# A decoder layer on one core: branch, output and query projections in three fp32r terms, norms between column groups

## What is computed

```python
def hybrid_mixer(h, ...):
    z = h @ p['w_in']                                   # q, k, v, gates, cq, ckv, kr, ga, gb
    ...                                                 # mLSTM branch gives hm
    y_a = hm @ p['w_branch_a']                          # 512 -> 1024
    ...                                                 # q_nope, k_nope, v from the latents
    o_lat = mla_attention(q_lat, q_rope, ckv, kr, ...)  # 8 heads; samples read 8192 cached tokens
    y_b = o_b @ p['w_branch_b']                         # 512 -> 1024
    y = (sigmoid(ga) * y_a + sigmoid(gb) * y_b) @ p['w_out']

def memory_attention(h, mem_k, mem_v, p):
    q = (h @ p['w_mq']).reshape(B, T, 4, 128)           # 1024 -> 512
    ...                                                 # softmax over 256 memory tokens
    return o @ p['w_mo']

def decoder_layer(x, ...):
    mem_k, mem_v = memory_kv(mem_prompt)                # norm of 256 memory rows, two 1024 -> 512
    x = x + rms_norm(hybrid_mixer(rms_norm(x, g_pre_mix)), g_post_mix)
    x = x + rms_norm(memory_attention(rms_norm(x, g_pre_mem)), g_post_mem)
    x = x + rms_norm(swiglu_ffn(rms_norm(x, g_pre_ffn)), g_post_ffn)
```

## Time and profile before

| | us |
|---|---|
| median of 3 runs (lowest, highest) | 2562.77 (2562.18, 2566.25) |
| the profiled execution | 2563.37 |
| its span, first to last instruction | 2561.5 |
| TensorE busy | 2334.8 (91%) |
| VectorE, ScalarE, GpSimd busy | 950.8, 735.4, 320.1 |
| mean granted TensorE clock | 0.961 of full |

### The profile page before, as it was taken

One profiled execution on the slowest core, in us unless ns is written; L12 is line 12 of the kernel. 1 busy time (PEld: TensorE's weight loads), 2 busy tenths in 40 slices (PEclk: granted clock), 3 DMA queues, 4 the chain that ended last, 5 costly groups with the idle time before them and its releaser, 6 DMA issues.

```text
span 2561.5 us, 36996 instructions
## 1 busy us (share of the span) xinstructions
PE 2334.8 (91%) x15757; PEld 1978.0 (77%) x15757; DVE 950.8 (37%) x1582; ACT 735.4 (29%) x1144; POOL 320.1 (12%) x384
## 2 busy tenths in 40 slices
PE   4999999999888899987999789958999999989994
PEld 4999899996444676665666456848999999989993
DVE  3352233334375554443110442464111111155556
ACT  5222222222343444434002112432111111144442
POOL 0000001102100477770020000000000000000000
PEclk9999999999899999998999899989999999999997
DMA  4123323332100577773141032021111111111121
GB/s 127 42 84 99 103 87 108 108 86 100 55 1 1 208 235 234 235 234 123 37 165 35 23 119 78 18 99 34 44 47 49 41 49 49 50 35 45 45 89 66
DMA packets 186468, 223.25 MB, mean 87 GB/s; under 512 B 18089, under 2 KB 148598, under 8 KB 185734
## 3 DMA queue, kind: packets, MB, share of 16 engines
q1 hardware_dynamic: 155238, 114.33, 14.5%
q0 software_dynamic: 31136, 107.56, 13.1%
HBM read 191.88 MB, written 29.98 MB: 87 GB/s over the span
## 4 chain that ended last, share of the span: by engine, by line
PE 77%; DVE 8%; POOL 5%; ACT 5%; issue 3%; DMA 2%; SPq 0%; POOLq 0%; ACTq 0%; DVEq 0%
PE ps L1410 21%; PE ps L937 17%; PE ps L1221 11%; PE ps L1610 10%; POOL mem L867 3%; POOL mem L868 2%; PE ps L1235 2%; PE ps L1240 2%; PE ps L1303 1%; DVE mem L2371 1%; PE ps L1107 1%; ACT mem L1831 1%; PE ps L1333 1%; DVE mem L2134 1%; DVE mem L2131 1%
## 5 line engine op out<-in xcount | busy, mean ns | idle before, releaser
L937 PE MATMUL ps<-stream_first,early_first 128*128 128x344 f32 x912 | 299.3, 328 | 4.3 <-DVE H_short L2087 3.0
L937 PE MATMUL ps<-H_short,early_first 128*128 128x344 f32 x912 | 294.7, 323 | 0.0
L937 PE MATMUL ps<-stream_first,ring_short 128*128 128x344 f32 x912 | 294.3, 323 | 0.0
L1221 PE MATMUL ps<-mem 128*128 128x344 f32 x960 | 282.5, 458 | 4.9 <-DMA mem<-w_out 4.3
L1221 PEld LDWEIGHTS ps<-mem 128*128 128x128 f32 x960 | 184.6, 193 | 102.5 <-issue 9.3
L1410 PE MATMUL ps<-stream_first,sel_short 128*128 128x344 f32 x1056 | 225.6, 322 | 16.0 <-DVE H_short L2664 16.0
L1410 PE MATMUL ps<-H_short,sel_short 128*128 128x344 f32 x1056 | 224.8, 321 | 0.0
L1410 PE MATMUL ps<-stream_first,ring_short 128*128 128x344 f32 x1056 | 223.4, 320 | 0.0
L1410 PEld LDWEIGHTS ps<-stream_first,sel_short 128*128 128x128 f32 x1056 | 178.2, 189 | 17.8 <-issue 13.4
L937 PEld LDWEIGHTS ps<-stream_first,early_first 128*128 128x128 f32 x912 | 174.9, 192 | 13.1 <-ACT mem L1740 6.1
L1410 PEld LDWEIGHTS ps<-H_short,sel_short 128*128 128x128 f32 x1056 | 179.5, 190 | 0.0
(11 more groups left out here) (422 smaller groups left out, 3389.8 us busy)
## 6 DMA issues: line engine op xcount, KB each, us to landing
ring_raw<-w_ffn_in SPq DMA_DIRECT2D x44, 512.0 KB, 3.6
ring_raw<-w_in SPq DMA_DIRECT2D x37, 512.0 KB, 3.8
ring_raw<-w_ffn_out SPq DMA_DIRECT2D x16, 704.0 KB, 4.5
branch_gates<-mem POOLq DMA_DIRECT2D x16, 516.0 KB, 4.6
mem<-branch_gates SPq DMA_DIRECT2D x2, 4128.0 KB, 14.5
chunks_apart<-mem POOLq DMA_DIRECT2D x12, 516.0 KB, 2.9
mem<-chunks_apart POOLq DMA_DIRECT2D x8, 768.0 KB, 5.7
residual_stream<-mem SPq DMA_DIRECT2D x8, 516.0 KB, 2.6
```

What stands on the lines that cost most here:

```text
L937: mm = pe.matmul(ps[:, bank, 0:TN], w[:, k], x[:, k, j * TN:(j + 1) * TN], start=(k == 0 and q == 0), stop=(k == KT - 1 and q == 2))
L1221: mm = pe.matmul(ps[0:m, s + j, 0:TN], w[:, k], x[:, j * TN:(j + 1) * TN], start=(k == 0), stop=(k == kts - 1))
```

## The change

- **a, b, out and mq become three-term fp32r products.** a, b and the first four out tiles use `product3` in thirds of 344 columns. Their inputs are split: Oo (for a) in the last decode unit, obT (for b) beside tiles 4 to 7 of a, the gated sum (for out) tile by tile behind the gates. The first two tiles of a stand ahead of the samples' product with w_uv, and their weights are loaded once the decode's values are done. The weights are split by ScalarE (`w_first`) and VectorE (`w_rest`).
- **The last four out tiles and mq run in column groups** of 384, 384 and 264: 24 products s = 0 to 23 (`group_product`), each one weight tile over one group with 24 matmuls; 0 to 11 are out, 12 to 23 mq. Their weights are split by ScalarE (`group_first`) and GpSimd (`group_rest`).
- **The norms run per group between these products.** ScalarE squares, GpSimd adds the squares (`add_square`), a matmul with ones sums them (`group_sum`), VectorE makes variance and reciprocal (`group_variance`), scales and adds the input (`add_input`), and later scales and splits the result (`stream_rest`).
- **Memory K and V stand behind mq**; kc, w_mv and vc are loaded later than before.
- **Three projection steps move into attention**: kn2 behind the first scores, kn3 and v2 behind the turns of units 0 and 1. Units 0 to 3 use one pair of banks.
- The one large SBUF tensor is allocated as two, and semaphores are renumbered.

```diff
-        N_A, N_B, N_OUT, N_MQ, N_MO, N_UP, N_DOWN = 0, 8, 16, 24, 28, 36, 80
+        N_A, N_B, N_OUT, N_MO, N_UP, N_DOWN = 0, 8, 16, 20, 28, 72
...
+        GROUP = [(0, 384), (384, 768), (768, T)]
+        SUMS = [("out", 0), ("in", 0), ("out", 1), ("out", 2), ("in", 1), ("in", 2)]
+        SUM_OUT = {4: 0, 8: 1, 12: 2}
+        SUM_IN = {7: 0, 13: 1, 17: 2}
+        QUADS = {5: (0, 0), 6: (0, 1), 9: (1, 0), 12: (1, 1), 14: (2, 0), 16: (2, 1)}
...
-        ATT = ["qr0", "qr1", "qn0", "rot0", "qn1", "rot1", "qn2", "qn3", "kn0", "kn1", "kn2", "kn3", "v0", "v1", "v2", "v3"]
+        ATT = ["qr0", "qr1", "qn0", "rot0", "qn1", "rot1", "qn2", "qn3", "kn0", "v0", "v1", "v3", "kn1", "kn2", "kn3", "v2"]
+        BESIDE = {0: "kn3", 1: "v2"}
...
+        def att_half(u):
+            return 1 if u < 4 else u % 2
...
@@ SyncE @@
+            sp.wait_ge(dec_values_done, NU)
+            for n in range(2):
+                load_w(N_A + n, w_a[:, :, n * P:(n + 1) * P])
             sp.wait_ge(pe_event, EV["o_T"])
...
+            for j in range(4):
+                load_group(j, w_o[:, :, (4 + j) * P:(5 + j) * P])
+            for j in range(4):
+                load_group(4 + j, w_q[:, :, j * P:(j + 1) * P])
...
+            sp.wait_ge(group_done, 24)
+            sp.dma_start(wmv, d["w_mv"][0].rearrange("(k p) m -> p k m", p=P)).then_inc(wmv_in, 16)
             for b in range(NB):
                 sp.dma_start(kc[:, b], kc_d[:, b]).then_inc(cache_keys_in, 16)
...
@@ GpSimd @@
+                pool.wait_ge(nrm_sq, SQ0 + n + 1)
+                if m:
+                    pool.tensor_tensor(acc, acc, gsq[n % 2][:, 0:w], ALU.add).then_inc(squares_added, 1)
...
+            for n in range(len(SQUARES)):
+                if n and SQUARES[n][2]:
+                    pool.wait_ge(squares_added, n)
+                add_square(n)
+                if n in (5, 8, 11, 12):
+                    group_rest((5, 8, 11, 12).index(n))
+                if SQUARES[n] in (("out", 2, 6), ("out", 2, 7), ("in", 1, 3), ("in", 1, 7)):
+                    group_rest(4 + (("out", 2, 6), ("out", 2, 7), ("in", 1, 3), ("in", 1, 7)).index(SQUARES[n]))
...
@@ TensorE @@
+            product3(N_A, H_rest[0:4], X_rest, ready=parts0, by=split_rest_ok)
+            product3(N_A + 1, H_rest[0:4], X_rest)
             pe.wait_ge(dve_event, EV["olat_ok"])
...
+            def group_product(s):
+                g, j = s // 12 * 4 + s % 4, s % 12 // 4
+                ...
+                if s >= 3:
+                    pe.wait_ge(group_evac, s - 2)
+                pe.wait_ge(group_rest_ok, g + 1)
+                for k in range(KT):
+                    if s >= 12 and s % 4 == 0:
+                        pe.wait_ge(split_rest_ok, parts0 + 16 + j * KT + k + 1)
+                    for q, (w, x) in enumerate(((ghi[g], first), (ghi[g], rest), (wlo[g % WSLOT], first))):
+                        mm = pe.matmul(ps[:, s % 3, 0:cols.stop - cols.start], w[:, k], x[k][:, cols],
+                                       start=(k == 0 and q == 0), stop=(k == KT - 1 and q == 2))
+                mm.then_inc(group_done, 1)
...
+            for s in range(24):
+                group_product(s)
+                if s in SUM_OUT:
+                    group_sum("out", SUM_OUT[s])
+                if s in QUADS:
+                    input_turn(*QUADS[s])
+                if s in SUM_IN:
+                    group_sum("in", SUM_IN[s])
...
@@ ScalarE, last decode unit @@
             for s in range(UPS):
                 dec_act(NB - 1, s, s == UPS - 1)
+                split_first(s, Alo[:, s], Oo[:, s])
+            act.wait_ge(pe_event, EV["o_T"])
+            w_first(0)
             act.wait_ge(dve_event, EV["wgt_arg"])
             act.activation(Wt, Wt, ACT.Exp, scale=SCALE)
             act.activation(Wself, Wself, ACT.Exp, scale=SCALE).then_inc(act_event, 1)
+            w_first(1)
...
@@ VectorE @@
             for s in range(UPS):
                 dec_dve(NB - 1, s, s == UPS - 1)
+                split_rest(s, Xlo[:, s], Oo[:, s], Alo[:, s])
...
+            group_variance("out", 0)
+            add_input(0, 0)
+            add_input(0, 1)
+            group_variance("in", 0)
+            group_variance("out", 1)
+            stream_rest(0)
+            add_input(1, 0)
+            add_input(1, 1)
+            group_variance("out", 2)
+            group_variance("in", 1)
+            add_input(2, 0)
+            stream_rest(1)
+            add_input(2, 1)
+            group_variance("in", 2)
+            stream_rest(2)
```

More of the change, by code:

```diff
@@ new lines, in group_sum @@
+            def group_sum(kind, j):
+                n = SUMS.index((kind, j))
+                c0, c1 = GROUP[j]
+                pe.wait_ge(squares_added, SQUARES.index((kind, j, KT - 1)) + 1)
+                if n:
+                    pe.wait_ge(nrm_var, NS0 + n)
+                else:
+                    pe.wait_ge(evac_act, 4)
+                acc = gacc_out[:, c0:c1] if kind == "out" else gacc_in[:, 0:c1 - c0]
+                pe.matmul(ps[:, 4, 0:c1 - c0], ones, acc, start=True, stop=True).then_inc(nrm_sum, 1)
@@ new lines, in _, with group_variance @@
+            for n in range(1, 2 * KT):
+                w_rest(n + 2)
+                gated(n)
+                if 4 <= n < 8:
+                    split_rest(n, ob_rest[:, n - 4], obT[:, n - 4], ob_first[(n - 4) // 2][:, n % 2])
+                if n >= KT + 2:
+                    sum_rest(n - KT - 2)
+            sum_rest(KT - 2)
+            sum_rest(KT - 1)
+            w_rest(N_OUT + 2)
+            w_rest(N_OUT + 3)
+            def group_variance(kind, j):
+                n = SUMS.index((kind, j))
+                r = grs_out if kind == "out" else grs_in
+                w = GROUP[j][1] - GROUP[j][0]
+                dve.wait_ge(nrm_sum, NS0 + n + 1)
+                step.step(dve.tensor_scalar(r[:, 0:w], ps[:, 4, 0:w], 1.0 / D, EPS, ALU.mult, ALU.add))
+                dve.reciprocal(r[:, 0:w], r[:, 0:w]).then_inc(nrm_var, 1)
@@ new lines, in add_input @@
+            def add_input(j, q):
+                cols = slice(*GROUP[j])
+                w = cols.stop - cols.start
+                dve.wait_ge(nrm_rstd, NS0 + SUMS.index(("out", j)) + 1)
+                for k in range(4 * q, 4 * q + 4):
+                    step.mark(dve.scalar_tensor_tensor(out=H[:, k, cols], in0=H[:, k, cols], scalar=gains[:, G_POSTMIX + k:G_POSTMIX + k + 1],
+                                                       in1=grs_out[:, 0:w], op0=ALU.mult, op1=ALU.mult))
+                step.join()
+                for k in range(4 * q, 4 * q + 4):
+                    dve.wait_ge(input_turned_again, j * KT + k + 1)
+                    dve.tensor_tensor(H[:, k, cols], H[:, k, cols], ps[:, X_BANK[k % 4], 0:w], ALU.add).then_inc(residual1_ok, 1)
@@ new lines, in stream_rest @@
+            def stream_rest(j):
+                cols = slice(*GROUP[j])
+                w = cols.stop - cols.start
+                r = grs_in[:, 0:w]
+                dve.wait_ge(nrm_rstd, NS0 + SUMS.index(("in", j)) + 1)
+                dve.wait_ge(residual1_ok, (j + 1) * KT)
+                for k in range(KT + 1):
+                    if k < KT:
+                        dve.scalar_tensor_tensor(out=A2[:, k, cols], in0=H[:, k, cols], scalar=gains[:, G_PREMEM + k:G_PREMEM + k + 1],
+                                                 in1=r, op0=ALU.mult, op1=ALU.mult).then_inc(group_raw_ok, 1)
+                    if k:
+                        split_rest(16 + j * KT + k - 1, sum_first[:, k - 1, cols], A2[:, k - 1, cols], Ahi[:, k - 1, cols])
```

667 lines of the change are left out of this document (411 added, 256 removed).

## The result

The changed kernel takes 2477.12 us (median of 4 runs, 2474.2 to 2478.61) beside 2564.51 us of the kernel before: ratio 0.9655, 95% interval 0.9637 to 0.9674. Forecast were 2468, between 2450 and 2500. The profiled execution took 2477.7 (span 2475.9), 85.7 less than that of before; the sum of the prediction was 95.9.

What follows compares the result with a forecast made beforehand. The prediction took TensorE, with 77% of the chain that ended last, to bound the kernel. Its terms -55.2 - 4.3 - 6.5 - 25.0 - 1.1 - 7.6 + 3.8 = -95.9 gave 2467.5, stated as 2468, range 2450 to 2500.

Steps and rivals of the forecast that it cites:

- Three terms: In a, b, out and mq, three fp32r matmuls replace each two-pass fp32 product: -55.2 us.
- Keys and later loads: After product 24, the later loads fit under memory K/V and the first scores: nothing lost.
- the second rival, late keys: Before the cross-attention scores, kc behind w_mv takes 43 us, 10 more than its cover: 2478; chance 0.12.
- mq to scores: Between mq and the first scores, the 1.1 us go, since memory V covers the last copies: -1.1.
- Attention: Three projection steps move between units 0 to 4, which take 22.0 us at full clock: -7.6.
- Decode: The decode moves earlier as a whole, but four splits in its last unit cost +3.8, bounds 1.3 and 8.
- the stretch of the norms between the groups: Between out and mq, norms run among column-group products: 84.75 us replaced by 59.8, with 13.9 of waits: -25.0.
- the walk: Queues followed in written order from the fourth out tile's end, VectorE and GpSimd not excluding each other: 2468; chance 0.57.
- the falling clock as an all-or-nothing rival: Waits between the groups drop TensorE to 1.2 GHz, 158 ns more a matmul: up to 2695; chance 0.03.
- first rival: In the column groups, GpSimd's adds and VectorE's two-SBUF-operand work exclude each other, 21 us more: 2489; chance 0.20.
- The fourth rival, exposed norms: Between out and mq the norms stay exposed; the 55.2 come, the 25.0 do not: 2493; chance 0.06.
- The start of a: After the decode, a's first tile starts at about 1195.1 in place of 1203.51, covering VectorE's chain: -6.5.

Runs made afterwards that it cites:

- e7: Changed kernel with GpSimd adding only 8 columns of the squares in place of 384 or 264: 2463.85 us, 0.9604 of the kernel before.
- e5: Changed kernel with post-norm row in PSUM, splits of a's input ahead of the decode's loop, four mq weight remainders on VectorE: 2467.45 us, 0.9617 of before.
- e2: Changed kernel with four more GpSimd adds of 384 columns on scratch beside the last stream_rest: 2482.49 us, 0.9662 of the kernel before.
- e4: Changed kernel with the attention part undone (kn2, kn3, v2 ahead of the first scores, two bank pairs alternating): 2489.42 us, 0.9691 of before.

## Why the prediction came out as it did

**Right.** *Three terms.* 72 x 12 matmuls of a, b and out and the 576 of the groups have the forecast durations: 174.5 ns at 384 columns and 121 at 264 by the starts in the timeline, 90.2 us in place of the 90.9 taken. The wait for w_out is gone. *Keys and later loads.* The chain has no DMA in it between mq and the first scores, though kc now lands a median of 11.6 us after issue in place of 9.2; the second rival, late keys, is out. *mq to scores* as forecast. *Attention.* Units 0 to 4 took 21.9 us (645.31 to 667.18), forecast 22.0, at full clock; the first gather behind attention came 9.1 us earlier (858.45 to 849.34) where 7.6 were forecast. *Decode.* Of these 9.1 the last decode values kept 5.8 (they end at 1174.05; before at 1179.84): 3.3 us for the splits, forecast 3.8; with the tail behind the values the early splits put it at about 5, inside the bounds of 1.3 and 8.

**Wrong: the stretch of the norms between the groups, 131.2 in place of 122.1.** The step that failed is the one that walked VectorE's chain at 0.61 us a scaling beside a busy GpSimd, and took its adds to be the only unknown there. Three things were off.

- *The exclusion is real.* Against the durations without adds (608 and 605 ns in e7, 0.55 us for a subtraction alone) the means of the changed kernel are these (busy us, mean ns):

```profile
L2820 DVE SCALAR_TENSOR_TENSOR mem_low<-mem_low 128x384 f32<-128x384 f32 x16 | 16.2, 1074 | 0.6 <-ACT mem_low L2076 0.6
L2836 DVE SCALAR_TENSOR_TENSOR mem_high<-mem_low 128x384 f32<-128x384 f32 x16 | 12.3, 781 | 0.0
L2715 DVE TENSOR_TENSOR sum_first<-mem_high,stream_first 128x384 fp32r<-128x384 f32 x16 | 12.0, 758 | 2.1 <-ACT stream_first L2013 2.0
```

  16 scalings of `add_input` lost 16 x (1074 - 608) ns = 7.5 us, 16 of `stream_rest` 2.8, and their subtractions 3.3: 13.6 us of VectorE. The rival had priced it at 21, by the share of time in which the engines would meet; they met less. And of the 13.6, e5 shows that 5 to 8 us were on the path, with what the clock and GpSimd's shorter queue gave back. The rest fell where VectorE waited anyway, as in e2. The Trainium skill (SBUF — State Buffer, section SBUF: two separate sides) says that a VectorE operation with two SBUF inputs and a GpSimd operation that reads SBUF lock each other out for a whole instruction, with no sharing of the bandwidth; the traces agree: beside 4.8 us of adds four scalings lost 3.1 us, and with one operand in PSUM they lost nothing. The sum by the rule, 2489, was too high, since it held every meeting for a loss on the path.
- *The adds are slower than in proportion*: 0.98 to 1.03 us alone at 384 columns and 0.75 at 264 (taken: 0.88 and 0.60), 1.07 from one to the next. The waits for the two sums were 3.5 and 4.7 us, forecast 1.6 and 2.7. In turn products 16 and 20 waited 0.8 us in all, forecast 5.5. So 15.6 us stand against 13.9, near each other by chance: with the exclusion mostly taken out (e5) the waits are 10.7.
- *VectorE alone is faster than walked*, which worked the other way. Undisturbed, four scalings take 2.19 us and four adds 1.95, 0.55 and 0.49 us each where 0.61 and 0.56 were taken. Of the 72.9 us in e5, 6.6 are remainders and 2.8 memory K's, so at most 63.5 stand against the 69.4 of the walk.
- *The clock.* Outside the waits TensorE took 131.2 - 15.6 = 115.6 us, forecast 108.2. By e7, 5.8 of these 7.4 are the grant (0.92 against 0.99). The prediction had the falling clock as an all-or-nothing rival with 3 in 100; it came in part, behind the long waits. In the table the stretch's clock mostly rises as the waits fall. But the waits don't settle it: in e4, with the same group code and the same 15.6 us of waits, it is 0.96 (columns as above, then the wait for the two sums):

```profile
1346.20:1474.60 128.40, 112.80 (x678) 105.67 (x677) 78.58 (x114) 54.98 (x108) 52.41 (x49) 0.96 0.16 52
...
PE ps L1550 <- POOL mem_low L986: 7.5, 2, 3.9
```

  Behind the first of these sums, after the same 3.5 us of waiting, the clock stayed at 1.00 there (1383.2 to 1391.2), where the changed kernel had 0.63. So the cost of the clock behind the same waits varies by 2.7 us from one profile to another, and what decides it stays open.

So the measured time is nearer to the walk, 2468, than to the exclusion, 2489, and that the range held it is in part luck: errors both ways met in this stretch. What moved it off is the first rival's mechanism, at about a third of that rival's price, together with adds slower than taken and the clock. The fourth rival, exposed norms, is out: in the stretch that takes the place of the 84.75 us between out and mq, TensorE waits 15.6 us.

**A small one:** the first two tiles of a took 13.44 us in place of 11.4, since the first 4 us ran at 0.50: in the 17.8 us ahead of them TensorE is busy for 13.5 and has the same grant. The start of a was forecast to 0.5 us, and this was not looked at.

## What to carry to other kernels

When work is split over VectorE and GpSimd, list the operands: VectorE operations with two SBUF inputs and GpSimd's adds run one after the other, and putting the operand that they share into a PSUM bank made 24 operations immune, in a stretch that got shorter by 2.3 to 4.9 us in all. Price such a meeting by the part that stands on the path (here 5 to 8 of 13.6 us). After a wait of TensorE look at the granted clock as well: here it fell behind the longest waits in most profiles, and not in all. Work that fits under a stretch bound by something else (here the splits, under the gathers' pace) should stand early in it and not in its last unit, where nothing is left to cover it.

## What the runs showed of the hardware that was not expected

GpSimd's adds are held off too, by less: three of 384 columns took 3.60 us beside the scalings with two SBUF operands and 3.19 beside those with one. In attention, with the same instructions in all but e4, the clock from 760 to 800 us was 1.00 in three profiles (e4 is one) and 0.66 to 0.83 in eight, 5 to 9 us of the time; no edit goes with it, and what decides it stays open.
